# Two attentions of a fused network: heads taken in pairs on the two halves of the partitions

## The reference, cut to what matters

```python
# first block: every query attends to all 256 keys, head width 64 + 32 (rope), values 64 wide
s = einsum('bqhd,bkhd->bhqk', qn, k_nope) + einsum('bqhd,bkd->bhqk', qr, k_rope)
o = einsum('bhqk,bkhd->bqhd', softmax(s), v)
# second block, neighbourhood attention: 256 grid keys with a bias and a mask, 256 context keys
s_band = where(col_mask, einsum(q_r, k_band) + bias, NEG_INF)
s = concatenate([s_band, einsum(q_r, k_ctx)], axis=-1)      # 512 keys
p = softmax(s)
out = einsum(p_band, v_band) + einsum(p_ctx, v_ctx)
```

## Time and profile before

| | us |
|---|---|
| median of 3 runs | 2015.49 |
| lowest and highest | 2014.15, 2018.49 |
| the profiled execution's own time | 2017.46 |
| its span, first to last instruction | 2015.7 |
| first attention, from its first scores to the gate product behind it | 102.49 to 130.81 |
| neighbourhood attention, from its first scores to the product behind it | 1122.91 to 1182.26 |

### The profile page before, as it was taken

The page is one execution under the profiler, slowest core; times in us unless marked ns, Lnnn a source line. Parts: engine busy times, 40 slices in busy tenths (PEclk is TensorE's granted clock), DMA queues, the critical chain, the costliest instruction groups (busy, mean ns, idle before and its releaser), DMA issues.

```text
span 2015.7 us, 34549 instructions
## 1 busy us (share of the span) xinstructions
PE 1955.8 (97%) x13934; PEld 1775.3 (88%) x13934; DVE 1001.8 (50%) x2158; ACT 805.8 (40%) x872; POOL 1304.1 (65%) x311
## 2 busy tenths in 40 slices
PE   6999899999999999999999999899999999999998
PEld 4879788877767899999999678799999999999998
DVE  6766455765755554445336435453344334654112
ACT  3443343344445543344333323443344334334332
POOL 5727167766566677777774312387768776867784
PEclk9999899999999999999999899999999999999999
DMA  8537167778987556666664212266666665655442
GB/s 351 220 129 292 61 270 283 303 307 338 364 345 289 222 226 235 245 238 227 240 252 187 105 43 84 105 230 235 239 214 230 239 240 209 251 209 200 178 186 84
DMA packets 63957, 448.74 MB, mean 223 GB/s; under 512 B 7680, under 2 KB 8800, under 8 KB 9824
## 3 DMA queue, kind: packets, MB, share of 16 engines
q1 hardware_dynamic: 61888, 441.65, 58.1%
q10 hardware_dynamic: 1952, 5.44, 0.7%
HBM read 446.01 MB, written 1.05 MB: 222 GB/s over the span
## 4 chain that ended last, share of the span: by engine, by line
PE 53%; issue 23%; POOL 18%; DMA 4%; DVE 1%; ACT 1%; POOLq 0%; SPq 0%; ACTq 0%; DVEq 0%
POOL W L665 15%; PE bank L742 11%; PE bank L744 11%; PE bank L743 11%; DMA raw<-in_pages 3%; PE bank L1194 3%; PE bank L1262 3%; PE bank L1195 3%; PE bank L1202 2%; POOL YC L718 2%; PE bank L768 1%; PE bank L777 1%; PE bank L1137 1%; PE bank L788 1%; PE bank L807 1%
## 5 line engine op out<-in xcount | busy, mean ns | idle before, releaser
L665 POOL TENSOR_TENSOR W<-raw,W 128x2048 fp32r<-128x2048 f32 x220 | 1013.8, 4614 | 516.5 <-ACT W L1561 516.4
L742 PE MATMUL bank<-YH,W 128*128 128x256 f32 x1936 | 551.2, 285 | 1.1 <-POOL W L665 0.8
L744 PE MATMUL bank<-YH,W 128*128 128x256 f32 x1936 | 547.6, 283 | 0.0
L743 PE MATMUL bank<-YL,W 128*128 128x256 f32 x1936 | 547.6, 283 | 0.0
L1561 ACT ACTIVATE W<-raw 128x2048 fp32r<-128x2048 f32 x220 | 420.1, 1909 | 302.0 <-PE bank L744 275.6
L742 PEld LDWEIGHTS bank<-YH,W 128*128 128x128 f32 x1936 | 371.0, 192 | 3.9 <-POOL W L665 1.2
L743 PEld LDWEIGHTS bank<-YL,W 128*128 128x128 f32 x1936 | 371.2, 192 | 0.4 <-issue 0.2
L744 PEld LDWEIGHTS bank<-YH,W 128*128 128x128 f32 x1936 | 371.1, 192 | 0.0
L1916 DVE SCALAR_TENSOR_TENSOR bank<-mraw,CA,bank 128x256 f32<-128x256 f32 x696 | 328.9, 488 | 19.8
L2013 DVE TENSOR_TENSOR bank<-bank,SIL 128x256 f32<-128x256 f32 x110 | 47.6, 432 | 540.2 <-ACT SIL L1580 540.2
L742 PE MATMUL bank<-HH,W 128*128 128x256 f32 x880 | 249.7, 284 | 0.5 <-DVE HL L2015 0.4
(11 more groups left out here) (383 smaller groups left out, 3088.9 us busy)
## 6 DMA issues: line engine op xcount, KB each, us to landing
raw<-in_pages SPq DMA_DIRECT2D x284, 1024.0 KB, 4.8
mraw<-in_mpages SPq DMA_DIRECT2D x98, 1024.0 KB, 6.9
R<-in_pages SPq DMA_DIRECT2D x20, 1024.0 KB, 7.1
XR<-in_pages SPq DMA_DIRECT2D x12, 1024.0 KB, 6.1
R<-in_mpages SPq DMA_DIRECT2D x4, 1024.0 KB, 16.3
HT<-in_acts ACTq DMA_DIRECT2D x1, 1024.0 KB, 14.2
CT<-in_mpages SPq DMA_DIRECT2D x1, 1024.0 KB, 19.3
raw<-in_mpages SPq DMA_DIRECT2D x1, 1024.0 KB, 25.1
```

The costliest lines, as they stand in the source:

```text
L665: nc.gpsimd.tensor_tensor(WL[:, p % SLOTS, :], raw[:, p % SLOTS, :], WH[:, p % SLOTS, :].bitcast(f32), ALU.subtract).then_inc(s_lo, 1)
L742: mm(out, w[0], x[0], start=start, stop=False, skip_group_check=True)
L743: mm(out, w[0], x[1], start=False, stop=False, skip_group_check=True)
L744: return mm(out, w[1], x[0], start=False, stop=stop, skip_group_check=True)
```

## The change

In neighbourhood attention a step is now one block of 128 queries of a pair of heads, so there are 8 steps with two sides each. PE issues the two score products of a step one after the other, on partitions 0 to 63 and 64 to 127, into two banks; steps rotate over (0, 1) and (7, 6). Bank 6 otherwise holds the result of the modulation products, so PE waits at step 1 until that was taken. The value products of both heads of a pair are issued together, at every second step from 4 on, ahead of the transposes of that step, and alternate between the two output halves for each block of keys. Both sides are transposed after each other, with one bank for each side. ACT does copy, exponential, copy, exponential in a step (the copy ahead). DVE takes both maxima, then one reciprocal for two sums and both scalings. The page split by ACT comes at step 2 instead of step 3 (a step is now twice as large).

In the first attention the value products of two heads are issued together and alternate in the same manner, at every second step from 4 on, ahead of the transposes; ACT copies the transposed block ahead of the exponential.

```diff
+        NA_PAIRS = NA_H // 2
+        NA_N = NA_PAIRS * TB
         for a in range(NA_N + 3):
             if a < NA_N:
-                tile(f"sa{a}", 1, ((0, 1, 7)[a % 3],), None, free=lambda i, a=a: (sem("exp2"), a + 1))
+                for side in range(2):
+                    tile(f"sa{2 * a + side}", 1, (((0, 1), (7, 6))[a % 2][side],), None,
+                         free=lambda i, a=a, side=side: (sem("exp2"), 2 * a + side + 1))
             if a == 1:
                 tile("va1c", 1, (5,), "dve", VA_AT[1])
+            if a >= 4 and a % 2 == 0:
+                tile(f"oa{(a - 4) // 2}", 1, ((4, 5)[((a - 4) // 2) % 2],), "dve",
+                     own=(sem("oa_done"), (a - 4) // 2 + 1))
             if 2 <= a < NA_N + 2:
-                tile(f"pta{a - 2}", 1, ((2, 3)[a % 2],), None, free=lambda i, a=a: (sem("pt2"), a - 1))
-            if a >= 3 and (a - 3) % 4 == 1:
-                tile(f"oa{(a - 3) // 4}", 1, ((4, 5)[((a - 3) // 4) % 2],), "dve",
-                     own=(sem("oa_done"), (a - 3) // 4 + 1))
+                for side in range(2):
+                    tile(f"pta{2 * (a - 2) + side}", 1, ((2, 3)[side],), None,
+                         free=lambda i, a=a, side=side: (sem("pt2"), 2 * (a - 2) + side + 1))
...
-            def pv1(h):
-                if h % 2 == 0:
-                    opened(pe, f"o{h // 2}")
-                ps = bank(f"o{h // 2}")
-                pe.wait_ge(sem("pt1"), h + 1)
-                o = VD * (h % 2)
+            def pv1(pair):
+                ps = opened(pe, f"o{pair}")
+                pe.wait_ge(sem("pt1"), 2 * pair + 2)
                 for kb in range(TB):
-                    last = mm(ps[o:o + VD, 0:S], V1[:, kb, h * VD:(h + 1) * VD], PT1[:, h % 2, kb, :],
-                              start=(kb == 0), stop=(kb == TB - 1), skip_group_check=True)
-                return last
+                    for side in range(2):
+                        h = 2 * pair + side
+                        last = mm(ps[VD * side:VD * (side + 1), 0:S], V1[:, kb, h * VD:(h + 1) * VD], PT1[:, side, kb, :],
+                                  start=(kb == 0), stop=(kb == TB - 1), skip_group_check=True)
+                last.then_inc(sem("o1_done"), 1)
...
+                if h >= 4 and h % 2 == 0:
+                    pv1((h - 4) // 2)
                 if 2 <= h < H1 + 2:
                     turn1(h - 2)
-                if h >= 3:
-                    last = pv1(h - 3)
-                    if (h - 3) % 2 == 1:
-                        last.then_inc(sem("o1_done"), 1)
...
-                    h, qb = a // TB, a % TB
-                    o = HD * (h % 2)
+                    pair, qb = a // TB, a % TB
                     if a == 0:
                         pe.wait_ge(s_fa, tiles["qa", 1][2][1])
-                    ps = opened(pe, f"sa{a}")
-                    mm(ps[:, :], QA[o:o + HD, h // 2, qb * P:(qb + 1) * P], KA[o:o + HD, h // 2, :],
-                       start=True, stop=True).then_inc(s_tile, 1)
+                    if a == 1:
+                        pe.wait_ge(s_modev, MOD_AT["mixer"] + 2)
+                    ps = [opened(pe, f"sa{2 * a + side}") for side in range(2)]
+                    for side in range(2):
+                        rows = slice(HD * side, HD * (side + 1))
+                        mm(ps[side][:, :], QA[rows, pair, qb * P:(qb + 1) * P], KA[rows, pair, :],
+                           start=True, stop=True).then_inc(s_tile, 1)
                 if a == 1:
                     value(VA_AT[1], opened(pe, "va1c"), YC, s_page)
+                if a >= 4 and a % 2 == 0:
+                    pair = (a - 4) // 2
+                    if pair == 0:
+                        pe.wait_ge(s_fd, tiles["va1c", 0][2][1])
+                    ps = opened(pe, f"oa{pair}")
+                    pe.wait_ge(sem("pt2"), 4 * pair + 4)
+                    for kt in range(NKT):
+                        for side in range(2):
+                            h = 2 * pair + side
+                            last = mm(ps[HD * side:HD * (side + 1), 0:S], VA[:, kt, h * HD:(h + 1) * HD], PT2[:, side, kt, :],
+                                      start=(kt == 0), stop=(kt == NKT - 1), skip_group_check=True)
+                    last.then_inc(sem("oa_done"), 1)
                 if 2 <= a < NA_N + 2:
-                    turn2(f"pta{a - 2}", "pn2", a - 2, PROBA[:, (a - 2) % 4, :])
-                if a >= 3:
-                    b = a - 3
-                    h, qb = b // TB, b % TB
-                    if qb == 1:
-                        if h == 0:
-                            pe.wait_ge(s_fd, tiles["va1c", 0][2][1])
-                        if h % 2 == 0:
-                            opened(pe, f"oa{h // 2}")
-                        ps = bank(f"oa{h // 2}")
-                        pe.wait_ge(sem("pt2"), b + 1)
-                        o = HD * (h % 2)
-                        for kt in range(NKT):
-                            last = mm(ps[o:o + HD, 0:S], VA[:, kt, h * HD:(h + 1) * HD], PT2[:, h % 2, kt, :],
-                                      start=(kt == 0), stop=(kt == NKT - 1), skip_group_check=True)
-                        if h % 2 == 1:
-                            last.then_inc(sem("oa_done"), 1)
+                    for side in range(2):
+                        b = 2 * (a - 2) + side
+                        turn2(f"pta{b}", "pn2", b, PROBA[:, b % 4, :])
...
+                if h >= 2:
+                    copy1(h - 2)
                 if h < H1:
                     exp1(h)
-                if h >= 2:
-                    copy1(h - 2)
...
-                if a < NA_N:
-                    act.wait_ge(sem("mx2"), a + 1)
-                    c = 4 * (a % 2)
-                    soft_exp(PROBA[:, a % 4, :], bank(f"sa{a}")[:, :], ST[:, c:c + 1], ST[:, c + 2:c + 3])\
-                        .then_inc(sem("exp2"), 1)
-                if a >= 2:
-                    b = a - 2
-                    ps = filled(act, f"pta{b}")
-                    h, qb = b // TB, b % TB
-                    f(PT2[:, h % 2, :, qb * P:(qb + 1) * P], ps[:, :].rearrange("p (a t) -> p a t", a=NKT), ACT.Copy)\
-                        .then_inc(sem("pt2"), 1)
-                if a == 3:
+                for side in range(2):
+                    if a >= 2:
+                        qb = a % TB
+                        ps = filled(act, f"pta{2 * (a - 2) + side}")
+                        f(PT2[:, side, :, qb * P:(qb + 1) * P], ps[:, :].rearrange("p (a t) -> p a t", a=NKT), ACT.Copy)\
+                            .then_inc(sem("pt2"), 1)
+                    if a < NA_N:
+                        b, c = 2 * a + side, 4 * (a % 2) + side
+                        act.wait_ge(sem("mx2"), b + 1)
+                        soft_exp(PROBA[:, b % 4, :], bank(f"sa{b}")[:, :], ST[:, c:c + 1], ST[:, c + 2:c + 3])\
+                            .then_inc(sem("exp2"), 1)
+                if a == 2:
...
-                dve.wait_ge(sem("exp2"), a + 1)
-                link(v.reciprocal(ST[:, c + 2:c + 3], ST[:, c + 2:c + 3]))
-                v.tensor_scalar(PROBA[:, a % 4, :], PROBA[:, a % 4, :], ST[:, c + 2:c + 3], None, ALU.mult)\
-                    .then_inc(sem("pn2"), 1)
+                dve.wait_ge(sem("exp2"), 2 * a + 2)
+                link(v.reciprocal(ST[:, c + 2:c + 4], ST[:, c + 2:c + 4]))
+                for side in range(2):
+                    prob = PROBA[:, (2 * a + side) % 4, :]
+                    v.tensor_scalar(prob, prob, ST[:, c + 2 + side:c + 3 + side], None, ALU.mult).then_inc(sem("pn2"), 1)
```

More of the change, by code:

```diff
@@ L400, in build @@
                 tile(f"s{h}", 1, ((0, 1)[h % 2],), None, free=lambda i, h=h: (sem("exp1"), h + 1))
+            if h >= 4 and h % 2 == 0:
+                tile(f"o{(h - 4) // 2}", 1, ((3, 7)[((h - 4) // 2) % 2],), "dve",
+                     own=(sem("o1_done"), (h - 4) // 2 + 1))
             if 2 <= h < H1 + 2:
                 tile(f"pt{h - 2}", 1, ((2, 5)[h % 2],), None, free=lambda i, h=h: (sem("pt1"), h - 1))
-            if h >= 3 and (h - 3) % 2 == 0:
-                tile(f"o{(h - 3) // 2}", 1, ((3, 7)[((h - 3) // 2) % 2],), "dve",
-                     own=(sem("o1_done"), (h - 3) // 2 + 1))
         tile("g2", 1, (0,), "act", G_AT[2])
@@ L2440, in _, with maxa @@
             take_value("va1x", 0, 1, 0)
-            def maxa(a):
-                h, qb = a // TB, a % TB
-                ps = filled(dve, f"sa{a}")
-                c = 4 * (a % 2)
+            def maxa(a, side):
+                h, qb = 2 * (a // TB) + side, a % TB
+                ps = filled(dve, f"sa{2 * a + side}")
+                c = 4 * (a % 2) + side
                 link(v.tensor_tensor(ps[:, 0:S].rearrange("p (r c) -> p r c", c=GRID),
@@ L2453, in norma @@
                 c = 4 * (a % 2)
-                dve.wait_ge(sem("exp2"), a + 1)
-                link(v.reciprocal(ST[:, c + 2:c + 3], ST[:, c + 2:c + 3]))
```

(11 more changed lines are left out.)

1 line of the change is left out of this document (removed).

## The result

The changed kernel takes 1996.3 us (median of 4 runs, 1995.23 to 1998.3), the kernel before 2015.47 beside it (4 runs): a ratio of 0.9912, with an interval of 0.9896 to 0.9929. The forecast was 1995.5. The profiled execution has a span of 1995.2 us and a time of its own of 1996.98.

A forecast was written before the change was run, and what follows sets the result against it. The prediction took PE, busy 97% of the span, as the bound. Gains of 18.3 us in neighbourhood attention and 1.9 in the first attention took 2015.5 to 1995.3, said as 1995.5 us, range 1991 to 2001.

The forecast's parts named there:

- Score pairs: Neighbourhood attention: two score products on two row halves take 1.06 us, as one does; PE loses 8.5 us of work.
- Value pairs: Neighbourhood attention: value products of two heads on two column halves take 1.9 us instead of 3.74, saving PE 7.4 us.
- the rival without overlap: Both attentions: column halves do not overlap, value pairs stay 3.74 us in neighbourhood attention; time 2005 us, chance 0.11.
- the one with a price for alternation: Both attentions: each change of half empties the array, a neighbourhood value pair costs 6.1 us; time 2019.6 us, chance 0.04.
- DVE becomes the bound: Neighbourhood attention: DVE needs 6.8 us for two heads and PE 6.4, instead of 11.1 us before.
- The layout: Neighbourhood attention: 7.86 + 1.16 + 21.0 + 3.4 + 1.4 + 4.1 = 38.9, called 39.0 us, instead of 59.35.
- The stall at POOL's subtraction: Neighbourhood attention: a scaling waits behind POOL's subtraction of the split page for 4.1 us, bounds 0 and 4.5.
- The clock: Neighbourhood attention: a drop to 1.2 GHz may or may not come; 2 us added, making the stage 41.0 us.
- My layout of the old order at full clock: Neighbourhood attention before the change: 53.5 us by order; the 5.85 us left to 59.35 put down to half clock.
- The first attention: First attention: pairing value products gains 1.9 us, bounds -2.5 and +3.0, with the clock drop following a hole that stays.
- the loop: First attention: score, values, transposes, copy and exponential follow each other in a loop of 4.2 us for two heads.
- The sum: Whole kernel: gains of 18.3 us in neighbourhood attention and 1.9 in the first attention, 20.2 us together.

The follow-up runs named there:

- e4: Changed kernel, but in neighbourhood attention the second side's score product is issued behind the first side's transposes: 2001.5 us, ratio 0.9925.
- e5: Changed kernel, but the page split of step 2 of neighbourhood attention is done only behind its last step: 1994.28 us, ratio 0.9902.
- e3: Changed kernel, but in both attentions value products of a pair are issued all of one head, then all of the other: 1998.42 us, ratio 0.9914.
- e2: Kernel before with only the first attention changed, neighbourhood attention in its old order: 2012.51 us, ratio 0.9990.
- e9: Changed kernel, but both page splits are put behind their attention: 1992.2 us, ratio 0.9879.
- e7: Changed kernel, but the value products of neighbourhood attention alternate between the heads by twos: 1997.36 us, ratio 0.9913.
- e11: The changed kernel run once more, unaltered, as control: 1998.22 us, ratio 0.9911.
- e6: Changed kernel, but in the first attention ACT does the exponential ahead of the copy: 2000.95 us, ratio 0.9925.
- e1: Kernel before with only neighbourhood attention changed, the first attention in its old order: 1997.28 us, ratio 0.9918.
- e10: Changed kernel, but both page splits behind their attention and the first attention in its old order: 1989.48 us, ratio 0.9865.
- e8: Changed kernel, but the page split at the beginning of the first attention is done behind it: 1995.21 us, ratio 0.9905.

## Why the prediction was right

**Score pairs.** Four records in 1.06 us, as forecast from differential attention; e4 shows that it is the neighbourhood of the two that does it.

**Value pairs.** 1.88 us against 1.9, full overlap; the rival without overlap and the one with a price for alternation are out. The packing rule of the Trainium skill ("TensorE: Matmul & The Clock Gate", "Part 3: Packing small matmuls — row/col tiling"), that products on different tiles of the array run at the same time, held for two column halves of float32 products at 3.74 / 1.88 = 2.0 times.

**DVE becomes the bound.** 6.79 us for two heads against 6.8, in the one stretch between two value pairs that neither the stall nor the end of the stage touches.

**The stage.** The layout said 39.0 us at full clock, and it is 38.66, but two of its terms were off and cancelled. DVE's start at 9.03 us (1131.23 - 1122.20) was forecast as 9.02. From there to the end of the last scaling (1155.65) it is 24.4 us against 26.5: DVE did not wait for scores at all instead of 1.4 us (its 0.7 are two waits of 0.36 that end at 1123.36 and 1131.23, which the 9.02 holds), the stall was 3.9 instead of 4.1, and 12 blocks, 7 pairs of scalings and 2 output copies took 20.5 instead of 21.0. Behind the last scaling it is 5.2 us against 3.4, as the timeline after shows:

```profile
1154.77 0.88 DVE L2461 TENSOR_SCALAR R<-R,ST 128x512 f32<-128x512 f32 x2
1155.71 1.09 PE L1347 MATMUL bank<-IDENT,R 128*128 128x128 f32 x8
...
1156.40 1.09 ACT L1812 ACTIVATE R<-bank 128x512 f32<-128x512 f32 x2 [2.04 <-PE bank L1347]
1157.06 1.15 PE L1347 MATMUL bank<-IDENT,R 128*128 128x128 f32 x8 [0.25 <-ACT R L1812]
1157.75 1.09 ACT L1812 ACTIVATE R<-bank 128x512 f32<-128x512 f32 x2 [0.26 <-PE bank L1347]
1158.98 1.95 PE L1373 MATMUL bank<-R 128*64 128x256 f32 x16 [0.78 <-ACT R L1812]
```

I had put one transpose and one copy there; it is both sides of two steps, so four of each, with one bank for a side.

**The stall at POOL's subtraction** came in the place and at the size forecast, 3.9 us for 4.1, and e5 removed it. The Trainium skill, "SBUF — State Buffer", "SBUF: two separate sides", has the rule: DVE and POOL share one pair of ports, only some of DVE's instructions take it, and the one that starts first holds it for its whole instruction. The trace agrees: POOL started 0.45 us ahead (1136.23 against 1136.68), the scalings ended only behind it, and the exponentials of ACT beside them kept their 0.7 us. Nor does every instruction of DVE wait: two copies out of a bank beside POOL in the first attention took 0.69 us each (at 106.41 and 107.28, POOL ran from 106.09 to 110.61).

**The clock.** I had added 2 us for a drop that may or may not come; none came, in any of the eleven profiles of kernels with the pairs (those of e3 and e4 among them). The gain of the stage was 20.7 instead of 18.3. My layout of the old order at full clock, 53.5, was e2's 53.49, so the split of its 59.35 into order and clock was right too. But the forecast of the whole took all 59.35 as the starting point, and with it a drop of 5.9 us that e2's execution of the same order had not.

**The first attention** is the step that failed: "The drop to 1.2 GHz at 113.7 to 116.6 follows a hole that stays. Gain 1.9 us". The hole did stay, 3.2 us in both kernels, and the loop was right (4.33 us for two heads against 4.2, in e9). But the drop did not stay as it was: from 112.0 to 119.5 the mean clock is 0.54 after and 0.77 before, which is some 6.9 us at half clock against 3.4, and the stage gained 0.6 instead of 1.9. At full clock and with this hole the new order would need 24.2 + (3.2 - 2.0) = 25.4 us, and the old one 25.7 + 1.2 = 26.9, so the order is worth some 1.5 us and the longer half clock took 0.9 of it. In e5, which has the same first attention, the drop was as short as before (0.94 over the stage) and the stage took 26.5, a gain of 1.8. All other profiles of this order with the early split had 0.88 (e2, e3, e4, e7, e11 and the changed kernel), or 0.86 with e6's other order on ACT, and the three with the old order had 0.94 (before, e1, e10); why the new order mostly gets the longer drop is not known. I had taken the length of a drop for a property of the hole, and had given this stage no allowance for it, as I had in the other.

**The sum** was 20.2 us, and 19.2 came by the medians, 20.5 by the spans. The two misses, 2.4 too little in one stage and 1.3 too much in the other, went against each other. That the sum comes so near is in part luck: the profile from which it was reckoned lost 20.2 us to the clock (2015.7 x 0.010), the average execution of before 18.0. Over all executions the gain is 17.8 us (31 of before, 10 of the changed kernel), which lies in the range of the forecast, 2.4 under its middle.

## What to carry to other kernels

Products that fill half of the array, by rows or by columns, go in pairs next to each other in PE's stream; then the second half is free. For the column halves here it was enough to be within some four records of each other, whether they alternated or came by twos; for the row halves only the direct neighbourhood was tried. When PE stops being the bound, lay out the next engine instruction by instruction, and the drain behind its last instruction too: every transpose and copy of the last steps stands there. Once DVE is the bound, keep POOL's large elementwise work out of the stretch; moving one split behind the attention took 3.3 us off the stage here. Read the clock beside every median: between executions of the kernel before, what is put down to it ran from 12 to 26 us.

## What the runs showed of the hardware that was not expected

Two groups of eight records on the two column halves, issued one group after the other, overlap for about 1 of 3.7 us (e3). The records of the second group did not wait for the first group to be through: the first of them started 0.89 us after the pair began, beside the fifth record of eight.

Holes of the same length in PE's stream, 2.0 us, were followed by half clock in e10 and not in e8 and e9, and one hole of 3.2 us by half clock of different length in the profiles of before, of e5 and of the changed kernel. Neighbourhood attention kept 1.00 in all eleven profiles of the pairs, with PE busy 30.45 of 38.66 us in the changed kernel and 37.59 of 41.92 in e4, while the old order fell to half clock in the profile of before and not in that of e2 (47.60 of 53.49). What decides it stays open.
